# A two-layer diffusion trunk on one core: who adds the squares of a norm, where decay tables are made, and where modulation slabs stand

## The reference

```python
def _rmsnorm(x, g):
    y = x32 * lax.rsqrt(jnp.mean(x32 * x32, axis=-1, keepdims=True) + EPS)
    return y * g
def _modulation(cvec, w_mod, b_mod):            # six vectors: shift, scale, gate of two mixers
    m = jnp.einsum('bd,de->be', jax.nn.silu(cvec), w_mod) + b_mod
# one layer:
#   h = rmsnorm(x) * (1 + scale) + shift
#   z = h @ w_in        -> differential attention (with rotary embedding), neighbourhood
#                          attention, bidirectional retention, gates
#   x += gate * ((merged branches) @ w_out)
#   h = rmsnorm(x) * (1 + scale2) + shift2
#   x += gate2 * expert_choice_ffn(h)           # router, top k, 16 SwiGLU experts
# retention uses tables of exp(log_gamma * distance): d_in, d_cross, d_upd, g_chunk
# after the layers: y = rmsnorm(x, norm_final)
```

## Time and profile before

| | us |
|---|---|
| three runs, median | 2028.72 (2028.66 to 2030.94) |
| profiled execution | 2027.77 |
| its span, first to last instruction | 2025.70 |
| TensorE busy | 1867.7 (92%) |
| VectorE busy | 592.7 (29%) |
| ScalarE busy | 341.0 (17%) |
| GpSimd busy | 60.4 (3%) |
| moved by DMA | 552.38 MB, mean 273 GB/s |

### The profile page before, as it was taken

The page is one execution under the profiler, slowest core; times in us unless marked ns, Lnnn a source line. Parts: engine busy times, 40 slices in busy tenths (PEclk is TensorE's granted clock), DMA queues, the critical chain, the costliest instruction groups (busy, mean ns, idle before and its releaser), DMA issues.

```text
span 2025.7 us, 19626 instructions
## 1 busy us (share of the span) xinstructions
PE 1867.7 (92%) x8214; PEld 938.6 (46%) x8214; DVE 592.7 (29%) x1160; ACT 341.0 (17%) x787; POOL 60.4 (3%) x47
## 2 busy tenths in 40 slices
PE   5999999999999988888789999999999998888886
PEld 2565556555544333233345655565555343333323
DVE  1232447545221111101132324654533102010102
ACT  4022331100211101000141322210003010100102
POOL 1100000000000000000030000000000000000000
PEclk9999999999999999999999999999999999999998
DMA  9322272442589999999972221716225999999995
GB/s 389 152 94 88 84 307 78 166 166 77 208 365 428 429 429 429 430 429 428 426 309 94 83 88 57 287 42 249 110 102 245 396 429 428 429 429 428 429 429 243
DMA packets 53544, 552.38 MB, mean 273 GB/s; under 512 B 5840, under 2 KB 10832, under 8 KB 12240
## 3 DMA queue, kind: packets, MB, share of 16 engines
q1 hardware_dynamic: 49680, 548.51, 65.2%
q10 hardware_dynamic: 3776, 2.62, 0.4%
HBM read 546.91 MB, written 4.19 MB: 272 GB/s over the span
## 4 chain that ended last, share of the span: by engine, by line
PE 65%; DMA 29%; DVE 3%; ACT 2%; issue 1%; POOL 0%; SPq 0%; POOLq 0%; DVEq 0%; ACTq 0%
PE psum L943 12%; DMA ring<-in_w_up 12%; PE psum L1115 12%; DMA ring<-in_w_down 12%; PE psum L802 11%; PE psum L1027 6%; PE psum L804 6%; PE psum L1040 4%; DMA wide<-in_w_gate 3%; PE psum L397 2%; DMA ring<-in_w_gate 2%; PE psum L862 1%; PE psum L765 1%; PE psum L1095 1%; PE psum L1163 1%
## 5 line engine op out<-in xcount | busy, mean ns | idle before, releaser
L943 PE MATMUL psum<-hT,ring 128*128 128x384 f32 x768 | 255.8, 486 | 0.0
L802 PE MATMUL psum<-hT,ring 128*128 128x384 f32 x720 | 244.4, 493 | 7.2 <-ACT dense L1295 5.1
L1115 PE MATMUL psum<-dense 128*64 128x512 f32 x864 | 195.4, 596 | 30.8 <-DMA dense<-in_w_up 17.6
L1115 PE MATMUL psum<-ring,dense 128*64 128x512 f32 x832 | 188.2, 596 | 26.9 <-DMA ring<-in_w_gate 16.0
L943 PEld LDWEIGHTS psum<-hT,ring 128*128 128x128 f32 x768 | 145.7, 190 | 100.9
L802 PEld LDWEIGHTS psum<-hT,ring 128*128 128x128 f32 x720 | 135.8, 193 | 96.5 <-issue 6.6
L1115 PEld LDWEIGHTS psum<-dense 128*64 128x64 f32 x864 | 62.5, 137 | 153.6 <-issue 129.1
L1027 PE MATMUL psum<-dense,ring 128*128 128x384 f32 x384 | 131.9, 487 | 0.0
L1805 DVE TENSOR_TENSOR state<-state,psum 128x512 f32<-128x512 f32 x32 | 22.0, 688 | 373.2 <-PE psum L1115 335.2
L804 PE MATMUL psum<-ring,hT 128*128 128x512 f32 x288 | 126.5, 592 | 0.0
L1115 PEld LDWEIGHTS psum<-ring,dense 128*64 128x64 f32 x832 | 59.8, 137 | 140.7 <-issue 119.1
(11 more groups left out here) (211 smaller groups left out, 1680.2 us busy)
## 6 DMA issues: line engine op xcount, KB each, us to landing
ring<-in_w_up SPq DMA_DIRECT2D x32, 2048.0 KB, 38.2
ring<-in_w_in SPq DMA_DIRECT2D x60, 1024.0 KB, 8.6
dense<-in_w_up SPq DMA_DIRECT2D x30, 2048.0 KB, 40.0
ring<-in_w_down SPq DMA_DIRECT2D x30, 2048.0 KB, 40.1
dense<-in_w_gate SPq DMA_DIRECT2D x24, 2048.0 KB, 35.6
wide<-in_w_down SPq DMA_DIRECT2D x20, 2048.0 KB, 40.2
ring<-in_w_gate SPq DMA_DIRECT2D x20, 2048.0 KB, 36.7
wide<-in_w_gate SPq DMA_DIRECT2D x20, 2048.0 KB, 38.1
```

The source lines that it names most:

```text
L802: last = M.matmul(psum[:, bank, 0:T], ring[:, n % RING, k, cols], hT[:, k, :], start=k == 0, stop=k == KD - 1)
L943: last = M.matmul(psum[:, Z[1], 0:T], ring[:, n_gate % RING, k, (j % 4) * P:(j % 4 + 1) * P], hT[:, k, :], start=k == 0, stop=k == KD - 1)
L1115: last = M.matmul(psum[HALF * half:HALF * (half + 1), bank, :], lhsT(k), w[:, kk, half * SLAB:(half + 1) * SLAB], start=k == 0, stop=k == ...
```

## The change

It has four parts.

1. `ADDED` goes from 6 to 4 and a third square buffer is used (half of `tmp`): GpSimd adds squares 0 to 3 in three adds, TensorE multiplies squares 4, 5, 6, then the sum, then 7. ScalarE runs up to three squares ahead.
2. Start of a layer. In layer 0 group 0's first half stands before the transposes of slab (0,1), and a fourth group is begun early (`BEGUN`); slab `w_in` 0 takes the place of slab (0,3) in the ring and its first half is issued without a wait. In layer 1 slab (1,1) stands before `norm_sum`, slab (1,3) behind it, then group 0's first half, both transposes and group 1's first half; two groups are begun instead of three.
3. The decay tables: ScalarE makes them in three pieces, after reading groups 4, 5 and 6; VectorE's share stands between ropes 1 and 2.
4. Before the router `norm_sum` stands before the first modulation slab instead of behind it, and ScalarE does `inverse_rms` before it reads that slab.

```diff
-ADDED = 6
+ADDED = 4
+BEGUN = (4, 2)
+        squared = [square[:, 0, :], square[:, 1, :], tmp[:, 1, :]]
         START_FILL = [[("mod", 0, 0), ("modT", 0, 0), ("mod", 0, 2), ("modT", 0, 2), ("mod", 0, 1), ("modT", 0, 1), ("mod", 0, 3), ("modT", 0, 3)],
-                      [("mod", 1, 1), ("modT", 1, 1), ("mod", 1, 3), ("modT", 1, 3)]]
+                      [("mod", 1, 1), ("mod", 1, 3), ("modT", 1, 1), ("modT", 1, 3)]]
-            if FILL[f] in (("z", 0, 2), ("z", 1, 2)):
-                return O[0]
+            if FILL[f] in (("z", 0, 2), ("z", 0, 3)):
+                return O[FILL[f][2] - 2]
-        SLABS = [[("mod", j) for j in START_MODS[l]] + [("w_in", j) for j in range(9)] + ...
+        FIRST_SLABS = [[("mod", 0), ("mod", 2), ("mod", 1), ("w_in", 0), ("mod", 3)], [("mod", 1), ("mod", 3), ("w_in", 0)]]
+        SLABS = [FIRST_SLABS[l] + [("w_in", j) for j in range(1, 9)] + ...
# SP, start of the kernel
                 load_slab(0, 2)
+                load_half(0, 3, 0)
                 wait_slab_free(sp, 0, 0)
-                load_half(0, RING, 0)
-                load_slab(0, 3)
-                load_half(0, RING, 1)
+                load_slab(0, RING)
+                load_half(0, 3, 1)
# and the constants, keys and layer scalars of layer 0 are issued behind w_in slab 1, not ahead of it
# GpSimd
-                        G.tensor_tensor(sum_sq, sum_sq, square[:, k % 2, :], ALU.add).then_inc(sq_added, 1)
+                        G.tensor_tensor(sum_sq, sum_sq, squared[k % 3], ALU.add).then_inc(sq_added, 1)
# TensorE, norm_sum
-                    pe.wait_ge(sq_added, count(sq_added, (mixer + 1) * ADDED))
-                    M.matmul(psum[:, bank, 0:T], ones, sum_sq, start=True, stop=False)
                     for k in range(ADDED, KD):
+                        if k == KD - 1:
+                            pe.wait_ge(sq_added, count(sq_added, (mixer + 1) * ADDED))
+                            M.matmul(psum[:, bank, 0:T], ones, sum_sq, start=False, stop=False)
                         pe.wait_ge(sq_ready, count(sq_ready, mixer * KD + k + 1))
-                        last = M.matmul(psum[:, bank, 0:T], ones, square[:, k % 2, :], start=False, stop=k == KD - 1)
+                        last = M.matmul(psum[:, bank, 0:T], ones, squared[k % 3], start=k == ADDED, stop=k == KD - 1)
# TensorE, start of a layer (layer 0, then layer 1)
-                        fill(START_FILL[0][1:6])
+                        fill(START_FILL[0][1:5])
                         z_first_half(0)
+                        fill(START_FILL[0][5:6])
                         z_first_half(1)
                         fill(START_FILL[0][6:7])
                         z_first_half(2)
                         fill(START_FILL[0][7:8])
+                        z_first_half(3)
                     else:
+                        fill(START_FILL[layer][0:1])
                         norm_sum(TR[0], 0)
-                        fill(START_FILL[layer][0:1])
+                        fill(START_FILL[layer][1:2])
                         z_first_half(0)
-                        fill(START_FILL[layer][1:3])
+                        fill(START_FILL[layer][2:4])
                         z_first_half(1)
-                        fill(START_FILL[layer][3:4])
-                        z_first_half(2)
# TensorE, before the router
-                    fill(CHAIN_FILL[layer][0:1])
                     norm_sum(TR[0], 1)
-                    fill(CHAIN_FILL[layer][1:3])
+                    fill(CHAIN_FILL[layer][0:3])
# ScalarE, squares
-                        if 2 <= k < ADDED + 2:
-                            sc.wait_ge(sq_added, at(sq_added, mixer * ADDED + k - 1))
-                        elif k >= 2:
-                            sc.wait_ge(sq_summed, at(sq_summed, mixer * (KD - ADDED) + k - ADDED - 1))
+                        if 3 <= k < ADDED + 3:
+                            sc.wait_ge(sq_added, at(sq_added, mixer * ADDED + max(2, k - 2)))
+                        elif k >= 3:
+                            sc.wait_ge(sq_summed, at(sq_summed, mixer * (KD - ADDED) + k - ADDED - 2))
# ScalarE, decay tables: the same instructions in three functions
                     for g in range(Z_FIRST):
                         read_z(layer, g)
+                        if g == 4:
+                            decay_logs()
+                        if g == 5:
+                            decay_inside()
+                        if g == 6:
+                            decay_across()
# ScalarE, before the router
                     squares(layer, 1)
+                    inverse_rms(TR[0], 2)
                     read(CHAIN_FILL[layer][0:1])
-                    inverse_rms(TR[0], 2)
# VectorE: its share of the tables, unchanged, as decays()
                     for c in range(8):
+                        if c == 2:
+                            decays()
```

More of the change, by code:

```diff
@@ L473, in mod_parts @@
             return mod_columns[:, 32 * j:32 * j + 32]
-        SLABS = [[("mod", j) for j in START_MODS[l]] + [("w_in", j) for j in range(9)] + [("mod", j) for j in DENSE_MODS[l]]
+        FIRST_SLABS = [[("mod", 0), ("mod", 2), ("mod", 1), ("w_in", 0), ("mod", 3)], [("mod", 1), ("mod", 3), ("w_in", 0)]]
+        SLABS = [FIRST_SLABS[l] + [("w_in", j) for j in range(1, 9)] + [("mod", j) for j in DENSE_MODS[l]]
                  + [x for b in range(3) for x in (("w_in", 9 + 2 * b), ("branch", b), ("w_in", 10 + 2 * b))] + [("w_out", 0), ("w_out", 1)]
@@ L619, in buffer_free @@
                             wait_slab_free(sp, layer, SLABS[layer].index(FREED_LAST[(3, 5, 6, 7).index(i)]))
-                    first_w_in = len(START_MODS[layer])
+                    after_first = len(FIRST_SLABS[layer])
                     early_at = [SLABS[layer].index(x) for x in (("w_in", 13), ("branch", 2), ("w_in", 14))]
-                    for n in range(first_w_in + 1 if layer == 0 else 0, len(SLABS[layer])):
-                        if n == (first_w_in + 1 if layer == 0 else RING):
+                    for n in range(after_first if layer == 0 else 0, len(SLABS[layer])):
+                        if n == (after_first + 1 if layer == 0 else RING):
                             if layer == 0:
@@ L681, in add_squares @@
                     pool.wait_ge(sq_ready, at(sq_ready, mixer * KD + 2))
-                    G.tensor_tensor(sum_sq, square[:, 0, :], square[:, 1, :], ALU.add).then_inc(sq_added, 2)
+                    G.tensor_tensor(sum_sq, squared[0], squared[1], ALU.add).then_inc(sq_added, 2)
                     for k in range(2, ADDED):
@@ L794, in z_group @@
                         cols = slice(j * P, (j + 1) * P)
-                        begun = g < 3
+                        begun = g < BEGUN[l]
                         for k in range(KD // 2 if begun else 0, KD):
@@ L1318, in _ @@
                     else:
+                        read(START_FILL[layer][0:1])
                         inverse_rms(TR[0], 1)
@@ L1321, in _ @@
                         modulate(0, scale_mix, 0, 0, KD // 2)
-                        read(START_FILL[layer])
+                        read(START_FILL[layer][1:])
                     sc.wait_ge(mod1_ready, at(mod1_ready, 2))
                     modulate(0, scale_mix, 0, KD // 2)
[L1326 to L1347, removed]
+                    def decay_logs():
+                        sc.wait_ge(lam_sum, at(lam_sum, 1))
+                        A_.activation(lamb[:, 2:4], lamb[:, 0:2], ACT.Exp).then_inc(lam_exp, 1)
+                        sc.wait_ge(abs_ready, at(abs_ready, 1))
+                        link(A_.activation(decay_t[:, 1], decay_t[:, 0], ACT.Exp, scale=-1.0))
+                        A_.activation(decay_t[:, 2], decay_t[:, 1], ACT.Ln, bias=c_("one")).then_inc(ln_ready, 1)
@@ new lines, in decay_inside, with decay_across @@
+                    def decay_inside():
+                        sc.wait_ge(decay_ready, at(decay_ready, 1))
+                        for h in range(HEADS_C):
+                            A_.activation(in_decay[:, h], c_("below"), ACT.Exp, scale=decay[:, h:h + 1])
+                            last = A_.activation(bwd_decay[:, h], c_("above"), ACT.Exp, scale=decay[:, 4 + h:5 + h])
+                        last.then_inc(decay_exp, 1)
+                    def decay_across():
+                        for d, (row, col) in enumerate((("since", "k_until"), ("until", "k_since"))):
+                            for c in range(2):
+                                for i in range(2):
+                                    part = slice(64 * i, 64 * i + 64)
+                                    h = 4 * d + 2 * c + i
+                                    A_.activation(q_decay[part, d, c, :], c_(row)[part], ACT.Exp, scale=decay[part, h:h + 1])
+                            A_.activation(k_decay[:, d, :], decay[:, 4 * d:4 * d + 4], ACT.Exp, scale=c_(col))
+                        for i in range(2):
+                            part = slice(64 * i, 64 * i + 64)
```

(20 more changed lines are left out.)

10 lines of the change are left out of this document (2 added, 8 removed).

## The result

The changed kernel takes 2008.01 us in the median of four runs (2006.77 to 2008.39) against 2029.6 us for the kernel before in the same comparison: ratio 0.9892, 95% interval 0.9875 to 0.9909. The forecast was 2010.0 with a range of 2005.5 to 2017. The profiled execution took 2008.32 us (span 2006.1), 19.45 less than that of before; the forecast's sum was 18.7. Every execution used here had a granted clock of 0.99 or more, except one of run 5's ten (3248.64 us at 0.557), which hardly moves that run's median.

A forecast was written before the change was run, and what follows sets the result against it. The chain that ended last was 65% TensorE and 29% DMA, with time at both layer starts and the last norm. Gains 6.95 + 8.3 + 3.3 + 0.2 = 18.7 us off 2027.77 gave 2009.1, plus 0.95: 2010.0, range 2005.5 to 2017.

The forecast's parts named there:

- the 0.95 that I added for the median: Whole kernel: the median of the runs lies 0.95 us above the profiled execution, so 2009.1 became 2010.0 us.
- Layer 0, start: From the first slab to group 3's end: two extra norm products cost 1.29 us, reordering ends stalls; gain 6.95 us.
- What I said the gain contains: Layer 0's start: the gain includes the ScalarE stall and the slow clock, granted 0.52 in 44 to 46.
- Decay tables at nothing: Tables moved behind reads 4, 5 and 6 fit ScalarE's free time and cost nothing; at most 1 us a layer.
- Layer 1, start: From the last scatter product to group 3's end: slab (1,1) fills the wait for GpSimd's adds; gain 8.3 us.
- The last norm: After layer 1's scatter: the 3.6 us wait for adds shrinks, Ln at 2014.5 for 2017.82; gain 3.3 us.
- Routers: Norm before each router: Ln 0.64 us sooner, but ScalarE's slab read precedes modulation; gain 0.1 us each.
- The stream's slack: Expert loads behind the router slab: 5.8 us of slack less 3.2 leaves 2.6, so the later slab costs nothing.
- The port, rival (a): GpSimd's bias adds hold VectorE's rope 4, delaying rotation 6; up to 4 us a layer, about 2015; chance 0.09.
- my row: Layer 0's start: after 1.81 us idle the clock was granted 1.00, so short waits cost nothing.
- slow rival (c): Both layer starts: short waits bring TensorE down to 1.2 GHz and it stays there, 44 us more, 2054; chance 0.04.
- The rule that I set against the row: TensorE's clock: slow is the default and activity releases it, so several short waits together could keep it down.

The follow-up runs named there:

- run 5: Changed kernel with the decay tables put back ahead of the first of ScalarE's reads: 2022.22 us.
- run 1: Kernel before with the squares' part alone (GpSimd adds four, TensorE multiplies five, three square buffers): 2025.86 us, ratio 0.9969.
- run 6: Changed kernel with the modulation slab put back ahead of the router norm: 2011.78 us.
- run 10: Kernel before with idle products of unused results placed in TensorE's waits, no dependency changed: 2023.9 us, ratio 0.9967.
- experiment 2: Kernel before with the decay tables alone moved behind reads 4 to 6: 2021.37 us, ratio 0.9947.
- run 3: Kernel before with the order of the layer starts alone; three norm products, tables ahead of the reads: 2027.85 us, ratio 0.9979.
- run 4: Kernel before with the router norm alone moved ahead of the modulation slab, three products as before: ratio 0.999.
- run 7: Changed kernel with GpSimd adding six squares in layer 0's first norm and both router norms, four in the other two: 2005.66 us.
- run 11: Changed kernel with six squares added by GpSimd in the first four norms and four in the last: 2004.52 us, ratio 0.9869 to the kernel before.
- run 8: Changed kernel with GpSimd adding 7, 6, 6, 6, 5 squares in the five norms: 2005.5 us.

## Why the prediction was right, point by point

**The total: near in part by luck.** The profiled execution came out 0.75 us under the forecast's 2009.1. The 1.10 us before the first product, which I had not forecast, cover the 0.56 that layer 0's start missed; and the 0.95 that I added for the median, from the scatter of the kernel before, did not come: the changed kernel's median lies 0.31 under its profiled execution.

**Layer 0, start: 6.39 for 6.95.** The mechanism was right. Of the missing 0.56 us, 0.25 lie ahead of the Ln, which moved from 5.96 to 7.50 us after the first product, 1.54 and not 1.29. The price of the two products is not what was off: before, three norm products took 2.29 us, 0.35 more than three times 0.645; now five took 3.83, 0.60 more than five times. TensorE's first products are slow in every profile (the first slab's took 3.52 to 3.64 us, a later one's 1.93), and how long that lasts differs between executions of the same instructions: with five products the Ln stood 7.11, 7.50, 7.64 and 8.20 us behind the first product (run 1, the changed kernel, runs 5 and 6), with three 5.81 to 6.58 in six profiles. The prediction had no term for this. The other 0.3 lie in half group 0, which ended at 30.05, 1.61 us after chunk 2 was modulated (28.44) where I gave 1.29. From there on the rows follow the forecast's list: group 3 ended at 51.48, 21.43 us later (52.0 - 30.6 = 21.4 forecast).

What I said the gain contains was partly wrong. I counted the slow clock at 44 to 46 as a part of it; run 10 held the clock at 1.00 and this start got no shorter (44.74, all of the 0.62 ahead of the Ln), because the table stall set its end. It is the stall, together with the old order, that cost.

**Decay tables at nothing: right.** Rotation 1 to the output projection did not move (+0.04). Run 5 gives the cover's worth: 13.7 us if it is gone.

**Layer 1, start: 8.37 for 8.3.** The Ln starts 5.31 us after the last scatter product (5.4 forecast, 6.56 before). The new stretch was forecast well from its pieces; that the gain fits too is luck of the profile it is taken from, since the second profile of the kernel before has 40.75 us here, which would make it 10.1.

**The last norm: 3.31 for 3.3.** The new stretch, 3.67 us, is the forecast's (2014.5 - 2010.85 = 3.65). That the gain fits is luck here too: the kernel before's second profile has 7.87 us for this stretch, and experiments 2 to 4, whose code is the same there, 7.56 to 7.88, with the clock falling earlier. Run 10 splits it: 1.1 us clock, 2.2 the adds.

**Routers: 0.23 and 0.22 for 0.1 each.** ScalarE's read of the slab does set the modulation's start, as the timeline shows: read at 542.25, after the slab's product, and modulation behind it.

```profile
540.37 0.58 ACT L1262 ACTIVATE rs<-psum,const 128x384 f32<-128x384 f32 x1 [1.93 <-PE psum L726]
...
542.25 0.60 ACT L1279 ACTIVATE kcT<-psum 128x512 f32<-128x512 f32 x1 [0.75 <-PE psum L769]
...
542.75 2.72 ACT L1270 ACTIVATE hT<-hT,modT,scale_ffn 128x128 f32<-128x128 f32 x6
```

**The stream's slack: right, 0.3 tighter than said.** Counted as in the prediction, by the DMA share (0.81 in the window ahead of the one shown), the preloads end about 2.3 us before the stream's first load is issued (2.6 forecast). The expert stages kept their length within 0.03 us. Single packets ran on until 1556.2, so little more could be taken from it:

```profile
1554.00:1556.00 2.00, 2.00 (x12) 0.72 (x10) 0.00 (x0) 0.00 (x0) 0.00 (x0) 1.00 0.08 25
...
1556.05 0.33 SPq L598 DMA_DIRECT2D dense<-in_w_down  x1
```

**The port, rival (a): real, and in layer 1 as near as I said.** In layer 0 rope 4 was caught, as forecast, and rope 5 as well:

```profile
69.23 9.41 POOL L703 TENSOR_TENSOR wide<-wide,const 128x2048 f32<-128x2048 f32 x2
...
69.64 4.62 DVE L1618 TENSOR_TENSOR dense<-dense,tmp 128x256 f32<-128x256 f32 x1
...
74.77 4.15 DVE L1617 TENSOR_TENSOR dense<-dense,const 128x256 f32<-128x256 f32 x1
...
80.98 0.59 PE L824 MATMUL psum<-dense,const 128*128 128x256 f32 x2
```

VectorE gets its turn between GpSimd's two adds, so rope 4 ended at 74.26 (17.2 us after group 4, not 22) and rotation 6 at 80.98 had 6.7 us left instead of 2. In layer 1 two steps of rope 4 met one add each:

```profile
1058.03 9.17 POOL L703 TENSOR_TENSOR wide<-wide,const 128x2048 f32<-128x2048 f32 x2
1058.04 4.78 DVE L1617 TENSOR_TENSOR dense<-dense,const 128x256 f32<-128x256 f32 x1
...
1062.86 4.62 DVE L1618 TENSOR_TENSOR dense<-dense,tmp 128x256 f32<-128x256 f32 x1
...
1069.84 0.59 PE L824 MATMUL psum<-dense,const 128*128 128x256 f32 x2
```

It ended at 1067.48, 21.6 us after group 4 (about 22 forecast), and rotation 6 followed 2.4 us later. In run 3, where two steps of rope 0 met the same adds, it cost 0.9 us, and in run 5 0.7.

**The clock: my row did not bear the weight.** I argued that 1.81 us of idle time leaves the clock alone. Run 4 had the same place at 0.60. The changed kernel no longer has the long waits; the clock of its profile stayed at 1.00 through both starts, as in runs 6, 7 and 11, and its four runs lie within 1.6 us. That it can't fall there is not shown: in run 8 it did, around a wait of 1.32 us. The slow rival (c) did not come. The rule that I set against the row, in the Trainium skill (TensorE: Matmul & The Clock Gate, What's actually happening), that activity is what releases the slow clock, agrees with run 10, where unused products alone took 2.1 and 1.1 us off.

## What to carry to other kernels

Ask for each sum which engine comes late: handing terms from GpSimd to TensorE gained 3.3 us where TensorE sat waiting (2.2 without the clock, by run 10) and cost 0.9 to 1.3 in each of the three norms where it did not. Price edits of one stage together: the same move of the tables was worth 2.0 or 8.4 us in layer 0, by what stood around it. And a profile in which TensorE idles for some microseconds before products holds one draw of the clock's falls; stretches that differ between kernels are to be compared with a second profile of the same kernel first.

## What the runs showed of the hardware

- Around idle times of 1.3 to 3.6 us the granted clock sometimes falls to the 1.2 GHz level and sometimes later or not at all. At one place of the code it fell after 2.2 us (run 4) and did not after 1.8 and 2.4 (the kernel before, run 1); the last norm took 6.98, 7.87, 7.56 and 7.88 us in kernels where that code was the same. The kernel before ran in 2024.5 to 2036.2 us; with unused products in them (run 10) in 2023.4 to 2024.8.
- Two GpSimd adds back to back let a waiting VectorE instruction through in between: each rope step was held for at most one add (4.62 of 9.41 us, 4.78 of 9.17).
- The time from the first expert product to the last scatter product is 442.2 to 442.7 us in all thirteen profiles and both layers, wherever it starts.
- The first slab's product, TensorE's first work, took 3.52 to 3.64 us in all thirteen profiles; a later one at granted clock 1.00 took 1.93.
